# Expert values: the last 512 columns of the second token half, summed on VectorE from gathered rows instead of by TensorE

## The reference, cut to what matters

```
def block(args):
    xb, eb, gb = args
    act = gelu(einsum('tkd,td->tk', u_tab[eb], xb), approximate=False)
    return einsum('tk,tkd->td', gb * act, v_tab[eb])
```

## Time and profile before

| | |
|---|---|
| median of 3 runs | 2042.71 us (2042.55 to 2043.31) |
| span of the profiled execution, first to last instruction | 2047.0 us |
| mixer and router, to | about 578 us |
| U stage, to | 1339.2 us |
| V stage, to the last matmul | 2035.9 us |
| last norm's end and stores | 11.1 us |

### The profile page before, as it was taken

The page is one execution under the profiler, slowest core; times in us unless marked ns, Lnnn a source line. Parts: engine busy times, 40 slices in busy tenths (PEclk is TensorE's granted clock), DMA queues, the critical chain, the costliest instruction groups (busy, mean ns, idle before and its releaser), DMA issues.

```text
span 2047.0 us, 34143 instructions
## 1 busy us (share of the span) xinstructions
PE 2029.4 (99%) x11214; PEld 1764.3 (86%) x11214; DVE 1229.1 (60%) x2134; ACT 980.1 (48%) x1454; POOL 1115.0 (54%) x720
## 2 busy tenths in 40 slices
PE   9999999999999999999999999999999999999997
PEld 8998888889988888888888888888888888888886
DVE  1753121122888777558998988955555556655556
ACT  4544334445455565674444444444444444444443
POOL 6877778877788989888777777700000002200001
PEclk9999999999999999999999999999999999999999
DMA  8555656577688887776666666665555557556552
GB/s 291 169 152 170 193 172 215 177 205 196 155 182 192 191 186 173 176 187 166 162 160 161 162 162 164 164 226 185 198 192 190 200 187 278 191 191 260 187 198 86
DMA packets 153540, 381.35 MB, mean 186 GB/s; under 512 B 19808, under 2 KB 22496, under 8 KB 135680
## 3 DMA queue, kind: packets, MB, share of 16 engines
q1 hardware_dynamic: 153328, 380.32, 64.9%
q10 hardware_dynamic: 144, 0.13, 0.0%
HBM read 376.20 MB, written 4.19 MB: 186 GB/s over the span
## 4 chain that ended last, share of the span: by engine, by line
PE 91%; POOL 3%; issue 3%; DVE 1%; DMA 1%; ACT 0%; DVEq 0%; POOLq 0%; ACTq 0%; SPq 0%
PE ps L1604 33%; PE ps L1563 22%; PE ps L1564 11%; PE ps L1303 7%; PE ps L1304 7%; PE ps L1305 7%; PE ps L1545 3%; POOL w_lo L1217 2%; POOL u_lo L1255 1%; PE ps L1419 1%; DMA raw<-in_w_in 0%; PE ps L1299 0%; PE ps L1528 0%; PE ps L1437 0%; DMA v_raw<-in_peer_v 0%
## 5 line engine op out<-in xcount | busy, mean ns | idle before, releaser
L1563 PE MATMUL ps<-xT,u_hi 128*128 128x512 f32 x2048 | 727.5, 399 | 0.5 <-POOL u_lo L1255 0.5
L1255 POOL TENSOR_TENSOR u_lo<-u_t,u_hi 128x512 fp32r<-128x512 f32 x512 | 653.1, 1298 | 129.4 <-ACT u_hi L579 127.2
L1564 PE MATMUL ps<-xT,u_lo 128*128 128x256 f32 x2048 | 573.3, 280 | 0.0
L579 ACT ACTIVATE u_hi<-u_t 128x512 fp32r<-128x512 f32 x512 | 321.2, 632 | 360.1 <-DVE u_t L961 359.5
L1217 POOL TENSOR_TENSOR w_lo<-raw,w_hi 128x1024 fp32r<-128x1024 f32 x174 | 424.1, 2449 | 107.5 <-ACT w_hi L448 101.2
L1563 PEld LDWEIGHTS ps<-xT,u_hi 128*128 128x128 f32 x2048 | 384.7, 188 | 90.7 <-issue 0.6
L961 DVE STREAM_TRANSPOSE u_t<-u_raw 128x512 f32<-128x512 f32 x512 | 356.0, 702 | 105.8 <-PE ps L1564 72.8
L1564 PEld LDWEIGHTS ps<-xT,u_lo 128*128 128x128 f32 x2048 | 386.6, 189 | 0.0
L1604 PE MATMUL ps<-v_hi,m_hi 128*128 128x512 f32 x1024 | 317.9, 389 | 0.0
L1604 PE MATMUL ps<-v_hi,m_lo 128*128 128x512 f32 x1024 | 317.8, 389 | 0.0
L448 ACT ACTIVATE w_hi<-raw 128x1024 fp32r<-128x1024 f32 x175 | 184.8, 1059 | 271.7 <-PE ps L1305 265.2
(11 more groups left out here) (206 smaller groups left out, 2341.4 us busy)
## 6 DMA issues: line engine op xcount, KB each, us to landing
u_raw<-in_peer_u SPq DMA_DIRECT2D x512, 256.0 KB, 4.8
v_raw<-in_peer_v SPq DMA_DIRECT2D x126, 1024.0 KB, 4.9
raw<-in_w_in SPq DMA_DIRECT2D x111, 512.0 KB, 3.8
raw<-in_w_out SPq DMA_DIRECT2D x32, 512.0 KB, 4.8
raw<-in_w_peer_q SPq DMA_DIRECT2D x128, 128.0 KB, 3.4
x_again<-in_x SPq DMA_DIRECT2D x1, 2048.0 KB, 8.2
n_dram<-n_perm SPq DMA_DIRECT2D x1, 2048.0 KB, 8.1
n_again<-n_dram SPq DMA_DIRECT2D x1, 2048.0 KB, 9.3
```

Of the source, the lines that this page charges most:

```text
L579: act.activation(u_hi[:, slot(j, f), :], u_t[:, slot(j, f), :], ACT.Copy).then_inc(uhi_done, 1)
L1255: pool.tensor_tensor(u_lo[:, r, :], u_t[:, r, :], u_hi[:, r, :].bitcast(F32), ALU.subtract).then_inc(ulo_done, 1)
L1563: pe.matmul(acc, u_hi[:, r, c], xT[:, :, kt, :], start=kt == 0, stop=False)
L1564: ins = pe.matmul(acc[:, 0:T], u_lo[:, r, c], xT_hi[:, kt, :], start=False, stop=kt == KT - 1)
```

## The change

TensorE no longer computes bank 7, that is columns 1536 to 2047 of tokens 128 to 255. Each of these 128 tokens has 128 picks; with the token on the partition, VectorE adds for pick k the row part `v[pick k, 1536:2048]` times gate times activation into bank 7, 128 additions of 512 columns. What is needed for it:

- `place_picks` (VectorE, after the router): 11 small instructions that work out, for each token and pick, the place of its activation in a dense array in memory, and of its `v` row part. ScalarE writes both, and the gates, to memory.
- `act_dram`: the activations of the second token half. Those of tiles 0 to 63 are copied from `act_w` by four transfers of 1 MB (issued by ScalarE beside tiles 66 to 69). Those of tiles 64 to 127 come from a second Gelu instruction per tile of 128 columns, stored by SP (`far_store`, 64 transfers of 64 KB).
- GpSimd, after the U stage, gathers by indirect transfers, one per pick: an activation of 4 bytes for each of 128 tokens (`act_gather`), and a row part of 2 KB for each (`row_gather`), 256 indirect transfers in all, in chunks of five picks. A slot of `sp_rows` is filled again once VectorE has added it (`row_added`).
- VectorE adds a chunk of five in each group of four V tiles, from tile 16 to tile 117 (26 chunks, the last of three).
- The eight `h1_again` blocks are placed behind GpSimd's chunks 14 to 21. `h1_again` and `v_late_raw` change places, and SP waits for the last addition before it loads `v_late_raw`.
- The gates of the one-hot matmuls are read from PSUM as a scalar, not from a copy (`hot_cols`).
- `last_bank(1, 3)` moves from the end of the last norm's banks to its beginning.

```diff
@@ SP, U stage
+            def far_store(n, s):
+                sp.wait_ge(far_done, n + 1)
+                sp.dma_start(act_far[bass.ds(n, 1)].rearrange("i j t -> (i j) t"), far_act[:, s, :]).then_inc(far_out[s], 16)
...
+                    far_store(ii * 2 + s - 4 - P // 2, s)
@@ SP, V stage
-            for s in range(2):
-                sp.dma_start(v_late_raw[:, 2 * s:2 * s + 2, :].rearrange("p a b -> p (a b)"), v_rows[P - 2 + s].rearrange("j d -> j d")).then_inc(v_late, 16)
             with sp.Fori(P // 4 - 7, P // 4 - 1) as ii:
...
+            sp.wait_ge(row_added, P)
+            for s in range(2):
+                sp.dma_start(v_late_raw[:, 2 * s:2 * s + 2, :].rearrange("p a b -> p (a b)"), v_rows[P - 2 + s].rearrange("j d -> j d")).then_inc(v_late, 16)
@@ ScalarE
+                    act.activation(far_act[:, j % 2, :], z[:, P:T], ACT.Gelu).then_inc(far_done, 1)
...
+                    act.dma_start(act_near[:, 2 * K * j:2 * K * (j + 1)],
+                                  act_w[:, 0, P // 4 + 8 * j:P // 4 + 8 * (j + 1)].rearrange("p q i t -> p (q i t)")).then_inc(near_out, 16)
@@ VectorE, U stage
-                    ins = dve.tensor_scalar(hot_i[:, k, :], iota_ps, pick_ig[:, 0, t], pick_ig[:, 1, t], ALU.is_equal, ALU.mult)
+                    ins = dve.tensor_scalar(hot_i[:, k, :], iota_ps, pick_i[:, t], bank(5)[:, t], ALU.is_equal, ALU.mult)
@@ VectorE, V stage
+            def row_add(n, c):
+                dve.drain()
+                dve.wait_ge(row_in[c], n * 16 + 16)
+                dve.scalar_tensor_tensor(bank(7), sp_rows[:, c, :], sp_w[:, bass.ds(n * S_CHUNK + c, 1)], bank(7), ALU.mult, ALU.add).then_inc(row_added, 1)
...
                 dve.tensor_tensor(lo_v[:, n, :], raw_v[:, n, :], vh[0].bitcast(F32), ALU.subtract)
+                for chunk, c in added:
+                    row_add(chunk, c)
@@ GpSimd, V stage
+            def act_gather(n):
+                if n > 1:
+                    pool.wait_ge(act_in[n % 2], 16 * S_CHUNK * (n // 2))
+                for k in range(n * S_CHUNK, min(P, (n + 1) * S_CHUNK)):
+                    pool.indirect_dma_start(sp_w[:, k:k + 1], None, act_dram, bass.IndirectOffsetOnAxis(ap=sp_at[:, 0, k:k + 1], axis=0)).then_inc(act_in[n % 2], 16)
+            def row_gather(n):
+                for k in range(n * S_CHUNK, min(P, (n + 1) * S_CHUNK)):
+                    c = k % S_CHUNK
+                    if n:
+                        pool.wait_ge(row_added, k - S_CHUNK + 1)
+                    pool.indirect_dma_start(sp_rows[:, c, :], None, v_parts, bass.IndirectOffsetOnAxis(ap=sp_at[:, 1, k:k + 1], axis=0)).then_inc(row_in[c], 16)
...
+            act_gather(0)
+            act_gather(1)
+            for n in range(S_END):
+                row_gather(n)
+                if n + 2 < S_END:
+                    act_gather(n + 2)
+                if n > 13 and n < 22:
+                    h1_block((n - 14) // 4, (n - 14) % 4)
@@ TensorE, v_products
-                    for c in cs:
+                    for c in cs if (a, h) != (1, 1) else (0,):
@@ TensorE, last four tiles
-                for b in range(4):
+                for b in range(4 - a):
```

More of the change, by code:

```diff
@@ L385, in _ @@
                 load_v(s, s)
+            for s in range(2):
+                far_store(P // 2 - 2 + s, s)
             sp.wait_ge(spread_mm, P - U_SPREAD)
@@ L1066, in _, with place_picks @@
             route_pick(1, 1, 2, 1)
+            def place_picks():
+                i, j = ijg[:, 0, 1, :], ijg[:, 1, 1, :]
+                near, far, later, row = (pick_tmp[:, n, :] for n in range(4))
+                dve.wait_ge(tok_in, 16)
+                dve.drain()
+                dve.tensor_scalar(near, j, float(P * P // 2), tok[:, 1:2], ALU.mult, ALU.add)
+                dve.tensor_scalar(far, i, float(P * P), tok[:, 0:1], ALU.mult, ALU.add)
+                dve.tensor_scalar(later, i, float(P // 2), None, ALU.is_ge)
+                dve.tensor_scalar(row, j, float(D // COL), float(D // COL - 1), ALU.mult, ALU.add)
+                dve.drain()
+                dve.scalar_tensor_tensor(near, i, 4.0, near, ALU.mult, ALU.add)
+                dve.scalar_tensor_tensor(far, j, float(P), far, ALU.mult, ALU.add)
+                dve.scalar_tensor_tensor(pick_at[:, 1, :], i, float(P * D // COL), row, ALU.mult, ALU.add)
+                dve.drain()
+                dve.tensor_tensor(far, far, near, ALU.subtract)
+                dve.drain()
+                dve.tensor_tensor(far, far, later, ALU.mult)
+                dve.drain()
+                dve.tensor_tensor(pick_at[:, 0, :], far, near, ALU.add).then_inc(picks_done, 1)
+            place_picks()
             with dve.Fori(U_TURN // 6, U_SPREAD // 6) as ii:
@@ L1127, in _ @@
                 u_spread_tile(i // 6, i % 6, spreads=i > U_SPREAD + 1, weighs=i > U_SPREAD + 2)
-            with dve.Fori(U_UNROLL // 6, P // 6) as ii:
+            with dve.Fori(U_UNROLL // 6, 16) as ii:
+                for j in range(6):
+                    u_spread_tile(ii, j)
+            dve.wait_ge(near_out, 64)
+            with dve.Fori(16, P // 6) as ii:
                 for j in range(6):
@@ L1157, in _, with v_low_added @@
                 v_low(0, s, 0)
[L1158 removed]
+            dve.memset(bank(7), 0.0)
+            dve.wait_ge(picks_in, 32)
+            with dve.Fori(1, S_FIRST) as ii:
                 for s in range(4):
                     v_low(ii, s, 0)
[L1161 removed]
+            def v_low_added(ii, h, half, size=S_CHUNK):
+                n = ii - S_FIRST
+                weights(n, h, size)
+                for s in range(4):
+                    v_low(ii, s, half, added=[(n, c) for c in range(size) if c * 4 // S_CHUNK == s])
+            with dve.Fori(S_FIRST // 2, P // 16) as i2:
+                for h in range(2):
+                    v_low_added(i2 * 2 + h, h, 0)
+            with dve.Fori(P // 16, (S_FIRST + S_END) // 2 - 1) as i2:
+                for h in range(2):
+                    v_low_added(i2 * 2 + h, h, 1)
+            v_low_added(S_FIRST + S_END - 2, 0, 1)
+            v_low_added(S_FIRST + S_END - 1, 1, 1, P - (S_END - 1) * S_CHUNK)
+            for ii in range(S_FIRST + S_END, P // 4 - 1):
                 for s in range(4):
```

109 lines of the change are left out of this document (85 added, 24 removed).

## The result

The changed kernel takes 1985.78 us (median of 4 runs, 1982.38 to 1987.02) against 2043.01 us for the kernel before on the same chip. The ratio is 0.9719, with a 95% interval of 0.9705 to 0.9733. A second series gave 1984.1 us and 0.9705 (0.9692 to 0.9719). So the change brings 57 to 60 us, where 75 were forecast: 1968 us, with 1955 to 2032 as the range. The direction came out as written, and so did the mechanism that was to bring the gain. Of the written signs of "right" two did not come: the V stage is 630 us long and not near 612, and TensorE is not busy throughout. Four terms of the sum were off in size, and the largest of them can be got back (run c1).

What follows compares the result with a forecast made beforehand. TensorE's matmuls were taken to bound the kernel. 87.0 us saved, less 2 + 4 + 1 + 1 + 1.5 + 0.65 + 2 of costs, gave -74.9 us: 2042.7 to 1968 us, range 1955 to 2032 (8 in 10).

Steps and rivals of the forecast that it cites:

- what goes: V stage: three matmuls fewer in each of 128 tiles, 384 x 0.2267 = 87.0 us saved, the others unchanged.
- the additions are hidden: V stage: VectorE's work takes 15.7 of 19.04 us a group, so matmuls hide the additions with 2.4 us to spare.
- GpSimd keeps up: V stage: ten indirect transfers at 1.3 us each take 13 of 19.04 us a group, cost 0.
- DMA share: V stage: loads and gathers take the DMA engines 13.5 to 19.2, mean 16 of 19.04 us; share near 0.8.
- the load behind the 4 MB: V load behind the 4 MB for `h1_again`: lands about 14 us after issue, costing up to 4 us, taken as 2.
- the `h1_again` blocks: GpSimd, beside eight chunks: a block of two instructions adds 2.7 us, 15.7 of 19.04 us, cost 0.
- the end: Last four tiles and last norm: up to 1.5 us of wait, 0 to 1 for `v_late_raw` loads, 0.65 for the norm.
- the U stage: Before the V stage: activation stores 4 us, scalar from PSUM 1 us, `place_picks` 1 us.
- Gathers that set the pace: Rival: GpSimd's indirect transfers pace the V stage, costing from 2.0 us each, 2085 us at 2.5; 13%, of this 9% slower.
- The port: Rival: gathers slow VectorE's two-input subtractions, 3.1 us over in 26 groups, 82 us, about 2050; 8%, half of it slower.
- The DMA engines: Rival: gathered pieces at 0.147 us each fill the DMA engines, 2.6 us over in 26 groups, about 2035 us; 5%.
- The remaining matmuls: Rival: TensorE's remaining matmuls run slower because VectorE writes PSUM beside them, about 2000 us; 2%.

Runs made afterwards that it cites:

- c1: The change with the eight `h1_again` blocks behind GpSimd's last gather and their 4 MB loaded as four spread 1 MB pieces; 1971.8 us, ratio 0.9648.
- d1: The change without its gathers and VectorE's additions, bank 7 staying zero; 1966.3 us, ratio 0.9617 to the kernel before.
- d3: The change with each activation gather issued twice, so 15 indirect transfers a chunk instead of 10; 2083.5 us, ratio 1.0173.
- e2: The change with GpSimd's eight `h1_again` blocks moved behind its last gather; 1981.3 us, ratio 0.9689 to the kernel before.
- c2: Like c1, but with `v_late_raw` loaded behind tiles 124 and 125 instead of ahead of them; 1970.0 us, ratio 0.9645.
- d2: The change with TensorE computing bank 7 again (24 matmuls a tile), no gathers or additions, preparation kept; 2046.7 us, ratio 1.0009.
- e1: The change with the 4 MB for `h1_again` split into four 1 MB loads, each behind four V tiles; 2001.8 us, ratio 0.9791.

## Why the prediction was right, and where its sizes were off

**Right: what goes.** 384 matmuls of 0.2267 us are gone, and no other became slower wherever nothing waits. In d1, with everything out that the additions need, the gain is 2045.2 - 1966.3 = 79 us of the 87.

**Right: the additions are hidden, where nothing is late.** One takes 0.755 us, two stand 0.97 us apart (0.83 forecast), and VectorE has 471 of 630 us. The slack of about 2.4 us is real: waits for a row of up to 2 us elsewhere cost nothing, and 2.13 + 2.68 us in one tile made a pause of 2.28. Where a load is late, two additions stand between its landing and TensorE (at 1660 us).

**Right: GpSimd keeps up, with less room.** 1.3 us per indirect transfer was taken; it is 1.17 and 1.26 us plus 0.30 to the next, so 1.5. GpSimd waits 122.5 us for VectorE's additions, the picture that was written down as the sign of "right". d3 shows how near the edge is.

**Right: DMA share.** 16 of 19.04 us (0.84) forecast, 0.78 to 0.85 measured in the windows with gathers and no other load.

**Off: the load behind the 4 MB.** "The load behind them lands about 14 us after its issue, so up to 4 us; I take 2." It landed after 16.6 us; without gathers (d1) it was 12.6, and the stall 1.8 us. And the time until TensorE notices is not 11.5 us: the load was issued 14.1 us before TensorE ran dry, and from its landing to the first matmul it was 4.7 us, so 9.4. In d1, where no additions stand there, the 4.7 are 2.8. Together a pause of 7.2 us. The sum also had no term for the clock, which made 9.3 of it. c1 takes this stall away. Size of the error: 7 us.

**Off: the `h1_again` blocks.** "Beside eight chunks a block of two instructions adds 2.7 us, 15.7 of 19.04." It adds 5.2 in the mean because of its drain, on 15.2 us of gathers: 20.4, over the 19.04. With two long drains rows came late twice. The forecast had 2 us for late rows, and it is 8 to 9, the half clock behind the pauses included. Error: 6 us. e2 shows that the blocks do it.

**Off: the end.** "Up to 1.5 us of wait" and "0 to 1" for the loads of `v_late_raw`, 0.65 for the norm. In the V stage it is 3.6 us (6.6 in the second trace, where the last of three pauses is followed by half clock). The loads of tiles 124 and 125 land 7.9 and 7.0 us after their issue, and ScalarE waits for both. The tail is 13.4 us long instead of 11.1:

```profile
1972.60 0.16 DVE L1307 SCALAR_TENSOR_TENSOR small<-small 128x1 f32<-128x1 f32 x1 [3.05 <-POOL small L1344]
```

Error: 4 to 7 us. VectorE waits there for GpSimd, which is late by its one drain of 2.27 us. In the four runs with the blocks behind the gathers and the order of the tail kept (d1, e2, c1, c2) that drain takes 0.14 us and the tail 11.6 to 11.8 us, which is the old 11.1 and the forecast's 0.65. So the term for the norm was right, and the drain was missing.

**Off, the other way: the U stage.** 6 us were taken for stores, scalar and `place_picks`; d2 says 1.8. VectorE in the window 900 to 1330 (the earlier trace rows have 900 to 1300):

```profile
L1021 DVE STREAM_TRANSPOSE u_t<-u_raw 128x512 f32<-128x512 f32 x265 | 186.4, 705 | 24.2 <-DMA u_raw<-in_peer_u 12.2 <-PE ps L1721 11.7
L1173 DVE TENSOR_SCALAR hot_i<-ps,pick_i 128x128 f32<-128x128 f32 x256 | 86.1, 397 | 0.0
```

The scalar from PSUM costs 3 ns an instruction (397 against 394). The waits for `u_raw` rose from 7.0 to 12.2 us, but they took the place of waits for TensorE (15.4 to 10.2 in the window of the earlier trace rows).

Put together: -75 + 7 + 6 + 5 - 4 = -61 us, where the medians give -57 and -60. What remains lies within what one profile differs from the next: the V stage began between 1333.8 and 1340.6 us in kernels whose code before it is the same.

**Luck in the range.** The load behind the 4 MB was given 0 to 4 us and cost 9.3, the late rows 0 to 6 and cost 7.9, and the end went over its terms too. That the time still lay under the forecast's 1990 is owed to the U stage, whose terms reached up to 14 us for the PSUM scalar alone and came to nearly nothing. The chances are also added wrongly: 72 + 4 + 3 + 3 + 2 is 84, not 80, and with 3 and 18 for the rest they make more than 100.

**The rivals.** Gathers that set the pace: not at ten a chunk, yes at fifteen. The port: the gathers do not slow VectorE (L1246 takes 1.23 us beside them, 1277 ns in the mean with the blocks). It works the other way: gathers wait for VectorE, see below. How much of the cost of gathers this is, no run tells apart. The DMA engines: full only beside the 4 MB and at the last loads. The remaining matmuls: unchanged.

## What to carry to other kernels

When an engine takes over work under a full TensorE, price the in-order queues of its helpers with all that stands in them, drains included: here a block between gathers cost 5.2 us and its two instructions 2.6, and an operation that waits for a load holds every gather behind it. A large load that was just hidden before is not hidden once the tile time shrinks and other transfers share the engines: spread it, and first move whatever waits for it behind the urgent work (e1 without e2 lost 16 us, with e2 it gained 9). And a pause of TensorE can cost more than its length: the half clock behind the pauses of 7.21, 2.28 and 1.91 us added some 2 us each time.

## What the runs showed of the hardware

- An indirect transfer of 128 addresses holds GpSimd for 0.94 us or up to 2.02, and 0.30 us pass to the next. Between 1420 and 1660 us of the changed kernel there are 127. 58 began while no VectorE subtraction of `v_raw` and `v_hi` (L1246, L1252, two inputs from on-chip memory) was running, and took 0.94 to 0.97 us, also the 38 during which one then began. 69 began while one was running. But for one that began with it, they ended 0.80 to 0.83 us after the subtraction's end, or after the usual 0.94 to 0.96 us where that was later; so those that began early in it took 1.8 to 2.0 us. The subtractions stayed at 1.22 to 1.28 us in both cases. So here the gather waits and VectorE does not, where beside GpSimd's own arithmetic VectorE was slowed. The Trainium skill (SBUF — State Buffer, Who interferes with whom) states that the order of issue decides who waits when both want the shared ports. On the gathers that began inside a subtraction the trace agrees; that a subtraction would wait for a gather begun before it, the trace does not show.
- The first drain on GpSimd behind indirect transfers takes 0.96 to 5.43 us in the changed kernel's eight blocks, up to 6.8 in c2, and 2.27 us in the changed kernel's last norm, 76 us after the last gather. There and in e2 each further drain, with no gather since the one before, takes 0.14 or 0.15 us. It isn't a wait for the data: in e1, where the block had waited 25.4 us and the last gather had been issued long before, the drain still took 5.07 us. What it waits for stays open.
- After pauses of TensorE of 7.21, 2.28 and 1.91 us the granted clock was 0.50 during the next 3.4 to 3.7 us of its work. Pauses of 1.46 and 1.64 us with 0.97 us of work between them left it at 1.00. The same two pauses at the end of c1 (1.41 and 1.64 us) and e2 (1.60 and 1.64) did not: there it fell to 0.50 within the second, and stayed for 5.4 and 5.9 us of the work behind it. What makes the difference, no run here tells.
